# A one-core transformer-block kernel: its step-size projection turned round into four column groups, with a copy and nine pick products behind it

## What is computed

```python
proj = h @ lw['w_in']                      # h: 1032 tokens x 1024 features
...
dt = jax.nn.softplus(s[..., W + SSM_CONV_DIM:].astype(f32) + lw['ssm_dt_bias'].astype(f32))
...
xdt = x.astype(f32) * dt[..., None]
da = dt * a
```

## Time and profile before

| | us |
|---|---|
| median of 3 runs | 1847.2 (1845.36 to 1851.68) |
| the profiled execution, its own time | 1845.79 |
| its span, first to last instruction | 1844.1 |
| TensorE busy | 1629.5 (88%) |
| DVE busy | 657.2 (36%) |
| ACT busy | 369.1 (20%) |
| POOL busy | 189.6 (10%) |
| mean granted TensorE clock | 0.935 of full speed |

### The profile page before, as it was taken

The page is one execution under the profiler, slowest core; times in us unless marked ns, Lnnn a source line. Parts: engine busy times, 40 slices in busy tenths (PEclk is TensorE's granted clock), DMA queues, the critical chain, the costliest instruction groups (busy, mean ns, idle before and its releaser), DMA issues.

```text
span 1844.1 us, 21447 instructions
## 1 busy us (share of the span) xinstructions
PE 1629.5 (88%) x8042; PEld 1036.0 (56%) x8042; DVE 657.2 (36%) x1237; ACT 369.1 (20%) x653; POOL 189.6 (10%) x297
## 2 busy tenths in 40 slices
PE   5999889999499989989989999999999769969960
PEld 3666556676277767767767776566535533323310
DVE  2003039823443343434534433477402311101107
ACT  3100230022113133131331314300002211101102
POOL 2003600002110100101101000000000001101100
PEclk9999989969799999999999999999999769989995
DMA  4111101108201111011110112155401077665536
GB/s 159 34 34 46 38 12 35 46 4 89 75 32 42 47 43 46 32 43 46 43 47 32 43 46 94 50 227 214 174 0 67 26 319 288 246 266 215 214 143 274
DMA packets 38070, 181.25 MB, mean 98 GB/s; under 512 B 5400, under 2 KB 5720, under 8 KB 29024
## 3 DMA queue, kind: packets, MB, share of 16 engines
q1 hardware_dynamic: 21808, 113.94, 17.9%
q0 software_dynamic: 16176, 66.06, 10.9%
HBM read 336.81 MB, written 38.21 MB: 203 GB/s over the span
## 4 chain that ended last, share of the span: by engine, by line
PE 82%; DMA 7%; DVE 5%; issue 3%; ACT 2%; SPq 0%; POOL 0%; DVEq 0%; ACTq 0%; POOLq 0%
PE ps L449 35%; PE ps L777 7%; PE ps L834 6%; PE ps L746 6%; DMA arena<-in_w_gu 3%; PE ps L848 3%; PE ps L691 3%; DMA scr<-h_rows,idx 2%; PE ps L600 2%; PE ps L605 2%; PE ps L583 2%; PE ps L610 2%; PE ps L499 1%; PE ps L765 1%; PE ps L467 1%
## 5 line engine op out<-in xcount | busy, mean ns | idle before, releaser
L449 PE MATMUL ps<-arena,wring 128*128 128x344 f32 x2304 | 695.9, 452 | 1.2 <-ACT arena L930 1.2
L449 PEld LDWEIGHTS ps<-arena,wring 128*128 128x128 f32 x2304 | 424.2, 190 | 203.8 <-issue 4.3
L834 PE MATMUL ps<-arena,scr 128*32 128x512 f32 x1280 | 152.0, 627 | 24.4 <-DMA arena<-in_w_gu 24.4
L1670 POOL DMA_DIRECT2D gate_scratch<-stage x96 | 52.2, 544 | 802.5 <-ACT stage L983 544.2
L777 PE MATMUL ps<-arena 128*128 128x512 f32 (+1 forms) x288 | 125.6, 594 | 1.2 <-DVE arena L1442 1.2
L746 PE MATMUL ps<-arena,wring 128*128 128x344 f32 x384 | 111.2, 451 | 0.0
L834 PEld LDWEIGHTS ps<-arena,scr 128*32 128x32 f32 x1280 | 41.4, 115 | 120.5 <-issue 104.7
L746 PEld LDWEIGHTS ps<-arena,wring 128*128 128x128 f32 x384 | 72.5, 189 | 38.6
L777 PEld LDWEIGHTS ps<-arena 128*128 128x128 f32 (+1 forms) x288 | 50.7, 178 | 71.0 <-issue 69.2
L848 PE MATMUL ps<-arena,scr 128*32 128x512 f32 x640 | 75.3, 612 | 15.2 <-issue 13.8
L891 ACT ACTIVATE arena<-ps 128x344 f32 (+1 forms) x63 | 28.7, 457 | 259.2 <-PE ps L449 241.9
(11 more groups left out here) (385 smaller groups left out, 1869.8 us busy)
## 6 DMA issues: line engine op xcount, KB each, us to landing
arena<-in_w_gu SPq DMA_DIRECT2D x160, 1024.0 KB
arena<-in_w_dn SPq DMA_DIRECT2D x80, 1024.0 KB
wring<-in_w_all SPq DMA_DIRECT2D x61, 512.0 KB, 3.6
gate_scratch<-stage POOLq DMA_DIRECT2D x96, 172.0 KB, 2.2
arena<-gate_scratch POOLq DMA_DIRECT2D x4, 2064.0 KB, 10.0
scr<-gate_scratch POOLq DMA_DIRECT2D x4, 2064.0 KB, 8.9
arena<-y_rows SPq DMA_DIRECT2D x16, 512.0 KB, 9.8
scr<-in_x_t SPq DMA_DIRECT2D x2, 2064.0 KB, 12.1
```

The source lines that it names most:

```text
L449: mm = pe.matmul(ps[:, c, 0:CW], wring[:, slot, k, :], H[:, k, chunk(c)], start=k == 0, stop=k == KT - 1)
L834: mm = pe.matmul(ps[S * j:S * (j + 1), i % 2, :], XT[i % 2][:, k * P + S * j:k * P + S * (j + 1)], GU[j][:, k * 2 * HID:(k + 1) * 2 * HID] ...
L1670: pool.dma_start(gate_scratch[:, bass.ds(base + g, 1), chunk(c)], stage[:, c:c + 1, :]).then_inc(sem(f"gate_out{c}"), 16)
```

## The change

The step-size products are made the other way round. The weights are padded from 4 to 32 columns (28 of zeros) and are stationary; the tokens move, 344 at a time. Feature block k = 2g + s goes to column group g (g from 0 to 3), which sums its two blocks s = 0 and 1 into partitions 32g to 32g + 31 of banks 3 to 5, one bank for a chunk: 24 products. Row 32g + h of a bank then holds a quarter of head h's sum. ACT copies the three banks to `stage` in one instruction. Nine products, one for each block of tokens, take 128 tokens of `stage` as the stationary operand and a constant `pick20` (128x20, its first 4 columns used) as the moving one: it has a one where partition mod 32 is the head, so each product adds the four quarters and puts tokens on partitions, in bank 6 as before. These nine stand behind the second L524. L517's first product now waits for the copy (`dt_ev`), and ACT's gate tile 0 and DVE's bias addition wait for the picks (`dt_mm` 5). `w_r` is no longer loaded at the start into a buffer of its own, but behind the second load of x, into the space of `kk`, and `x_re` counts it (48 in place of 32). Several semaphores are merged (`k_std`, `norm_std` and `br_std` into `roots`, `bonus` into `rw_pre`, `cum` into `c_ready`, `shift_saved` into `lerp`, `smp_done` into `pre_done`), with the counts shifted accordingly and the same instructions waited for.

```diff
-NSMALL_IN = 5 + 2 + 2 + 6
+NSMALL_IN = 4 + 2 + 2 + 6
...
+    put("pick20", np.eye(32)[i % 32, 0:20])
...
-        w_dt = sb("w_dt", [P, KT, 4])
-        w_r = sb("w_r", [P, KT, 20])
+        w_dt = sb("w_dt", [P, KT, 32])
...
+        w_r = kk[:, 0, 0:KT * 20].rearrange("p (k m) -> p k m", k=KT)
...
# TensorE, behind pairs(6, 10)
-            for n in range(9):
-                m = P if n < 8 else NSMP
-                for k in range(KT):
-                    mm = pe.matmul(ps[0:m, 6, 4 * n:4 * n + 4], H[:, k, n * P:n * P + m], w_dt[:, k, :], start=k == 0,
-                                   stop=k == KT - 1)
-            mm.then_inc(sem("dt_mm"), 1)
+            for c in range(NCH):
+                for s in range(2):
+                    for g in range(4):
+                        mm = pe.matmul(ps[32 * g:32 * g + 32, 3 + c, 0:CW], w_dt[:, 2 * g + s, :], H[:, 2 * g + s, chunk(c)],
+                                       start=s == 0, stop=s == 1)
+                        if s == 1 and c == NCH - 1:
+                            mm.then_inc(sem("dt_mm"), 1)
...
             for t in range(2):
                 pe.wait_ge(sem("rk_prod"), t + 1)
+                if t == 0:
+                    pe.wait_ge(sem("dt_ev"), 1)
                 if t == 1:
-                    pe.wait_ge(sem("bonus"), 1)
+                    pe.wait_ge(sem("rw_pre"), 1)
...
+            for n in range(9):
+                m = P if n < 8 else NSMP
+                mm = pe.matmul(ps[0:m, 6, 4 * n:4 * n + 4], STG[:, n * P:n * P + m], cc("pick20", 0, 4), start=True, stop=True)
+            mm.then_inc(sem("dt_mm"), 1)
+
             pe.wait_ge(sem("pool_ev"), 2)
             early_gates(6)
...
# ScalarE, behind the evictions of pairs(6, 10)
+            act.wait_ge(sem("dt_mm"), 4)
+            act.wait_ge(sem("c_ready"), 2)
+            A(stage[:, :, :], ps3(3), ACT.Copy).then_inc(sem("dt_ev"), 1)
...
+            act.wait_ge(sem("dt_mm"), 5)
             gate_tile(0)
...
# VectorE
-            dve.wait_ge(sem("dt_mm"), 1)
+            dve.wait_ge(sem("dt_mm"), 5)
...
-            dve.wait_ge(sem("x_re"), 32)
+            dve.wait_ge(sem("x_re"), 48)
...
# GpSimd
-            for dst, name in ((lora_w, "lora_w"), (pool_w, "pool_w"), (w_dt, "w_dt"), (w_r, "w_r"),
+            for dst, name in ((lora_w, "lora_w"), (pool_w, "pool_w"), (w_dt, "w_dt"),
...
             pool.dma_start(X2[0:NSMP, NTT - 1, :], ins["x"][TP:T, :]).then_inc(sem("x_re"), 16)
+            pool.dma_start(w_r, ins["w_r"]).then_inc(sem("x_re"), 16)
```

More of the change, by code:

```diff
@@ L73 @@
                   ("m_lev1_low", P), ("m_lev_low", 5 * P), ("imask", HD), ("rcount", 2 * 16), ("rwin", 2), ("rank4", 4),
-                  ("valid", NTT), ("tokv", 2 * NTT), ("count", P), ("restart", NE * NTT), ("part", 1), ("dummy", STEPS)]:
+                  ("valid", NTT), ("tokv", 2 * NTT), ("count", P), ("restart", NE * NTT), ("part", 1), ("pick20", 20), ("dummy", STEPS)]:
     CST[_name] = (_n, _w)
@@ L558, in _ @@
                 mm.then_inc(sem("bc_bc"), 1)
-            pe.wait_ge(sem("pre_done"), 1)
+            pe.wait_ge(sem("pre_done"), 2)
             with pe.Fori(0, NITER // 2) as i2:
@@ L868, in _, with inverse_root @@
             roots = [0]
-            def inverse_root(dst, src, name):
+            def inverse_root(dst, src):
                 roots[0] += 1
@@ L874, in inverse_root @@
                 act.wait_ge(sem("logs"), roots[0])
-                A(dst, dst, ACT.Exp, scale=-0.5).then_inc(sem(name), 1)
+                A(dst, dst, ACT.Exp, scale=-0.5).then_inc(sem("roots"), 1)
             for k in range(KT):
@@ L883, in _ @@
             act.wait_ge(sem("h_ready"), 1)
-            inverse_root(RS0, RS0, "norm_std")
+            inverse_root(RS0, RS0)
             def evac(n, m):
@@ L900, in _ @@
                 evac(2 * j - 5, 6 * j + 6)
-            act.wait_ge(sem("lerp"), 7)
+            act.wait_ge(sem("lerp"), 8)
             A(PR[0:32, S_LORA, PAD:], PR[0:32, S_LORA, PAD:], ACT.Tanh).then_inc(sem("lora_act"), 1)
@@ L915, in _ @@
                 act.wait_ge(sem("k_ss"), t + 1)
-                inverse_root(LL[:, t, :], LL[:, t, :], "k_std")
+                inverse_root(LL[:, t, :], LL[:, t, :])
             with act.Fori(6, 10) as j:
@@ L932, in _ @@
             for t in range(2):
-                act.wait_ge(sem("cum"), t + 1)
-                act.wait_ge(sem("bonus"), 2)
+                act.wait_ge(sem("c_ready"), t + 1)
+                act.wait_ge(sem("rw_pre"), 2)
                 A(TM[:, t, 0:TP], LL[:, t, 0:TP], ACT.Exp, scale=-DECAY_SCALE).then_inc(sem("dec_act"), 1)
@@ L956, in _ @@
             A(dsm[:, 2:4, 0:8], dsm[:, 2:4, 0:8], ACT.Exp).then_inc(sem("pre_act"), 1)
-            act.wait_ge(sem("pre_done"), 1)
+            act.wait_ge(sem("pre_done"), 2)
             def spread(i):
@@ L1044, in _ @@
             act.wait_ge(sem("br_var"), 1)
-            inverse_root(V5[:, 0, :], V5[:, 0, :], "br_std")
+            inverse_root(V5[:, 0, :], V5[:, 0, :])
             for t in range(2):
                 act.wait_ge(sem("br_var"), t + 2)
-                inverse_root(V2[:, t, :], V2[:, t, :], "br_std")
+                inverse_root(V2[:, t, :], V2[:, t, :])
             late_gates(g0 + 1)
             act.wait_ge(sem("br_var"), 4)
-            inverse_root(V4[:, 0, :], V4[:, 0, :], "br_std")
+            inverse_root(V4[:, 0, :], V4[:, 0, :])
             act.wait_ge(sem("ln_aff"), 2)
             for t in range(2):
-                A(V4[:, t, :], V3[:, t, :], ACT.Sigmoid).then_inc(sem("br_std"), 1)
+                A(V4[:, t, :], V3[:, t, :], ACT.Sigmoid).then_inc(sem("roots"), 1)
             late_gates(g0 + 2)
@@ L1135, in _ @@
             ts(as3(RS0), ps3(0), 1.0 / D, NORM_EPS, MUL, ADD).then_inc(sem("h_ready"), 1)
-            dve.wait_ge(sem("norm_std"), 1)
+            dve.wait_ge(sem("roots"), 1)
             for k in range(KT):
@@ L1145, in _ @@
             dve.wait_ge(sem("h_ready"), KT + 1)
-            nc.vector.tensor_copy(shift_out[:, :, :], PR[:, S_R:S_R + 7, PAD + TP - 1:]).then_inc(sem("shift_saved"), 1)
-            dve.wait_ge(sem("shift_saved"), 1)
+            nc.vector.tensor_copy(shift_out[:, :, :], PR[:, S_R:S_R + 7, PAD + TP - 1:]).then_inc(sem("lerp"), 1)
+            dve.wait_ge(sem("lerp"), 1)
             for t in range(7):
@@ L1152, in _ @@
                 stt(row(s), TM[:, t % 2, :], v("mu", t), row(s), MUL, ADD).then_inc(sem("lerp"), 1)
-            dve.wait_ge(sem("lerp"), 7)
+            dve.wait_ge(sem("lerp"), 8)
             for t in range(2):
@@ L1158, in _ @@
             for t in range(2):
-                dve.wait_ge(sem("k_std"), t + 1)
+                dve.wait_ge(sem("roots"), t + 2)
                 stt(kk[:, t, :], row(S_K + t, 0, TP), v("kkw", t), LL[:, t, 0:TP], MUL, MUL)
@@ L1174, in _ @@
             for t in range(2):
-                nc.vector.tensor_tensor_scan(LL[:, t, 0:TP], RESET, SG[:, t, 0:TP], 0.0, MUL, ADD).then_inc(sem("cum"), 1)
-            dve.wait_ge(sem("cum"), 2)
+                nc.vector.tensor_tensor_scan(LL[:, t, 0:TP], RESET, SG[:, t, 0:TP], 0.0, MUL, ADD).then_inc(sem("c_ready"), 1)
+            dve.wait_ge(sem("c_ready"), 2)
             dve.wait_ge(sem("lora_act"), 6)
@@ L1180, in _ @@
                 tt(row(S_CA + t), row(S_CA + t), row(S_CG + t), MUL).then_inc(sem("c_ready"), 1)
-            dve.wait_ge(sem("c_ready"), 2)
+            dve.wait_ge(sem("c_ready"), 4)
             link(nc.vector.tensor_copy(conv_h[:, :, :, CONVK - 1], rows(S_CA, 2, TP, T)))
@@ L1196, in _ @@
                 dve.wait_ge(sem("head_sum"), t + 3)
-                tt(as3(row(S_CA + t)), ps3(3), as3(row(S_V + t)), MUL).then_inc(sem("bonus"), 1)
+                tt(as3(row(S_CA + t)), ps3(3), as3(row(S_V + t)), MUL).then_inc(sem("rw_pre"), 1)
             for t in range(2):
@@ L1297, in _ @@
             link(tt(dsm[:, 6:8, 0:8], dsm[:, 6:8, 0:8], rows(S_Z, 2, TP, T), MUL))
-            tt(rows(S_Z, 2, TP, T), dsm[:, 6:8, 0:8], dsm[:, 8:10, 0:8], MUL).then_inc(sem("smp_done"), 1)
+            tt(rows(S_Z, 2, TP, T), dsm[:, 6:8, 0:8], dsm[:, 8:10, 0:8], MUL).then_inc(sem("pre_done"), 1)
             dve.wait_ge(sem("s_out"), 32)
@@ L1305, in _ @@
             nc.vector.memset(HT, 0.0).then_inc(sem("pre_done"), 1)
-            dve.wait_ge(sem("pre_done"), 1)
+            dve.wait_ge(sem("pre_done"), 2)
             with dve.Fori(0, NITER) as i:
@@ L1406, in _ @@
             ts(as3(V4[:, 0, :]), ps3(0), 1.0 / (2 * P), LN_EPS, MUL, ADD).then_inc(sem("br_var"), 1)
-            dve.wait_ge(sem("br_std"), 1)
+            dve.wait_ge(sem("roots"), 4)
             for t in range(2):
@@ L1410, in _ @@
             ins_.then_inc(sem("br_ready"), 1)
-            dve.wait_ge(sem("br_std"), 4)
+            dve.wait_ge(sem("roots"), 7)
             for t in range(2):
@@ L1420, in _ @@
                 tt(as3(row(O_RWKV + t)), as3(V1[:, t, :]), ps3(3 - 3 * t), MUL).then_inc(sem("br_ready"), 1)
-            dve.wait_ge(sem("br_std"), 6)
```

(15 more changed lines are left out.)

6 lines of the change are left out of this document (3 added, 3 removed).

## The result

The changed kernel takes 1804.51 us (median of 4 runs, 1801.96 to 1809.67) for 1847.4 before: a ratio of 0.9774, 95% interval 0.9751 to 0.9797. That is 42.9 us less where 23.1 were forecast (1824.0, range 1821 to 1827). The profiled execution took 1801.96, its span 1800.2. Two stretches hold the gain: the one the prediction worked on, and one it did not look at.

A forecast was written before the change was run, and what follows sets the result against it. TensorE, busy 88%, was taken to bound the kernel; its block of 39.96 us would take 16.9 (groups -21.5, copy +1.2, clock -3.4, picks +0.7), 23.1 us less: 1824.0 us, range 1821 to 1827.

The forecast's parts named there:

- The working for the block: TensorE's stretch from the step-size products to the gate products: 16.9 us for 39.96, 23.1 us less.
- The groups: The 24 new step-size products in four column groups, side by side: 48 records in 3.47 us, scaled from L834.
- The copy's gap: TensorE waits before L517 while ACT copies three banks to `stage`: 1.21 us more on the path.
- the first L517 with DVE's read: Behind the copy, at full clock: 3.39 us start to start, in place of 5.25.
- The first L524: Behind L517, ahead of the second L524: 2.96 us, as before.
- The picks: Nine products behind the second L524: 1.91 us, covering the idle time before the gates, net cost 0.7.
- DVE's idle time: Sign of being right: DVE's idle time before L1197, 33.28 us before, falls to about 11.
- The load of `w_r`: Moved behind x on POOL's queue: below 1.5 us with its issue, slack 8, so cost 0.
- The first rival: Clock falls in the new block: picks 3.4 for 1.9, together 2 to 5 us, 1826 to 1829; chance 0.24.
- The slower rival: Groups run in turn and hold the clock at half: block 52.2 us, 12.2 over before, 1859; chance 0.02.
- entering the four-group form: Start of the new step-size products: switching from full-width products costs nothing that L834's rows show.
- Who comes late next?: Everything behind the block: other engines shift with TensorE, order unchanged, so the whole gain is carried to the end.

The follow-up runs named there:

- a_serial: The changed kernel with all 24 step-size products in one column group instead of four; 1818.21 us, ratio 0.9837.
- b_merge: The kernel before, old step-size products kept, with pairs(0, 3) and pairs(3, 6) ahead of the SSD loop merged into pairs(0, 6); 1825.2 us, ratio 0.9882.
- b_split3: The kernel before, old step-size products kept, with the three loops ahead of the SSD loop cut into six of fewer turns; 1824.28 us.

## Why the prediction was wrong

The working for the block held. The groups took 3.73 us for 3.47, with a four every 0.29 us as scaled from L834, so that was the right row; the rest is the end of the last records, 0.45 us long each, which the sum left out. The copy's gap was 1.20 (372.22 to 373.42) for 1.21, the first L517 with DVE's read 3.48 for 3.39, the second 1.98 for 1.97. The first L524 took 2.95 for 2.96, the second 2.00 for 1.97. The picks took 1.81 for 1.91 and, as forecast, covered the wait for `pool_ev` 2. Together that is 17.15 for 16.9. DVE's idle time was 11.4 for "about 11", and L538 began 28.0 us behind the gates for 28. The load of `w_r` landed 2.2 us behind x (1276.2 against 1260.64 + 13.3) where 1.5 were allowed, well inside the slack of 8. The first rival did not come in the profile of the changed kernel, and did in a_serial's. The slower rival rested on a reading that the rows don't bear out: L489's first six 32-row records ran at full speed, in 1.97 us, and in the changed kernel the full-width L480 ran at half speed at the same place, in 3.78, so the half speed is not tied to the 32 rows.

At like positions of the loop the whole change is worth 20 to 25 us for 23.1. A closer test the runs don't allow: the changed kernel's own runs lie 8 us apart in one measurement and 15 in the other. In the two profiles everything outside the loop gives 22.2 us, which is near the forecast partly by luck, since +3.5, +2.9 and -4.2 us from parts that the sum put at nothing nearly cancel.

The prediction put nothing on entering the four-group form. The changed kernel's trace shows no wait there: the first group product starts before the full-width record ahead of it is over (368.42 against 368.49). Whether part of the 0.25 us by which the block is longer than the sum belongs to it is not shown.

The step that failed is the last sentence under "Who comes late next?": "From there on the order is unchanged, and I carry the whole gain to the end." The order was unchanged, but the code's place was not: the SSD loop behind it took 587.8 us for 609.5, because its code was no longer fetched anew at three jumps, some 7 us each. The prediction put that term at nothing without a reason. Its range left no room for it: it had bounds for transfers, clock and scatter, none for a loop that it had not read. The evidence stood in the trace of before. The chain had 4.03 us of "issue" inside a loop at 656 us, between two records of one line, and the page had 66 instruction packets. The prediction names neither, and does not ask what taking 39 products out of a program does to what lies behind them. The rival "faster than the sum" was missing altogether.

## What to carry to other kernels

When an edit changes the number of instructions ahead of a long hardware loop, read the loop too: idle time called "issue" just behind a jump back, and the count of instruction packets, say whether its code is fetched anew at each turn (here 4.03 us at the first jump and 66 packets, for none and 39). Then try the loop at two or three positions, by cutting or merging a loop ahead of it. That cost nothing measurable here (b_merge with one loop fewer took 1825.2 us, b_split3 with three more 1824.3), and it moved the time by 8 to 22 us, up to as much as the change itself. And compare two versions only at like positions; otherwise the place is measured and called the change.

## What the runs showed of the hardware

A TensorE loop of 1679 instructions ran with no instruction packets at its jumps at six positions and with nine a jump at four; a jump then cost 7.1 us (609.5 - 588.1, over three) or 2.7 (596.1 - 588.1). The packets were of 16 KB; 256 instructions in one is my estimate: the packet counts give 202 and 257, and starts 254 and 771 apart gave loops alike to 0.9 and 0.1 us. That seven such blocks are the bound is inferred from positions and not measured directly: the starts with packets at the jumps are 86, 89, 189 and 191 modulo 256, those without are 240 to 242 and 26 to 36.

Products of 32 stationary columns in one group, a quarter of the array, kept the granted clock at 1.00 for 14 us (a_serial). With 4 moving columns the clock was 0.50 from 2.7 us after they began, and L517's first six records behind them took 3.75 us, for 1.99 behind the groups and the copy. The 32-row products of L489 ran at either level, six records in 1.97 or 3.80 us.

Four column groups of 128x32 with 344 moving columns ran side by side: 48 records in 3.73 us, for 14.07 in one group.
